# Three attention stages: the product with the values turned round, bias and row extreme in one operation, order of the grouped units

## The reference

```python
# NA: each latent query sees an 8 x 16 window of keys with a position bias, and all 256 context keys
p = softmax_f32(jnp.concatenate([s_win * scale + rpb, s_ctx], axis=-1))
# GQA: each query sees all 1280 keys; 4 heads share one pair of keys and values
p = softmax_f32(concatenate([q @ k.T, q @ k_ctx.T]) * scale)
# FOX: causal over 1024 keys; decay terms ride in extra columns of q and k
out = p @ v        # in all three: probabilities times values, 64 columns per head
```

## Time and profile before

| | us |
|---|---|
| three runs | 4702.28, 4691.91, 4700.87; median 4700.87 |
| profiled execution, its own time | 4704.09 |
| its span | 4702.3 |
| PE busy over the span | 4112.0 (87%) |
| DVE, ACT, POOL busy | 2156.8, 1523.6, 815.8 |

### The profile page before, as it was taken

How to read it: one execution, slowest core, us unless ns; L and a number is a source line. 1 busy time by engine, 2 the same in 40 slices (tenths; PEclk the granted TensorE clock), 3 DMA queues, 4 the chain that set the end, 5 groups by cost and what they waited for, 6 DMA issues and landing times. The chain is left out here.

```text
span 4702.3 us, 74174 instructions
## 1 busy us (share of the span) xinstructions
PE 4112.0 (87%) x29857; PEld 3383.3 (72%) x29857; DVE 2156.8 (46%) x3952; ACT 1523.6 (32%) x3236; POOL 815.8 (17%) x725
## 2 busy tenths in 40 slices
PE   8999797998989985898887879997895988999998
PEld 2789787997889872787776724446794766888786
DVE  3233375344522228677777764475313553111234
ACT  2111254655521117333333350005212553221133
POOL 0000353100100661434444460001000000000000
PEclk9999898999999997999999979998897989999999
DMA  8233432102332566212222050214224132111122
GB/s 321 74 102 115 111 80 60 32 18 92 126 99 92 191 221 250 62 35 49 49 49 49 22 188 25 76 49 170 91 92 165 49 119 72 49 45 49 38 89 69
DMA packets 291264, 439.23 MB, mean 93 GB/s; under 512 B 76980, under 2 KB 210708, under 8 KB 286399
## 3 DMA queue, kind: packets, MB, share of 16 engines
q1 hardware_dynamic: 290664, 429.81, 28.9%
q10 hardware_dynamic: 288, 5.07, 0.3%
HBM read 315.76 MB, written 124.03 MB: 94 GB/s over the span
## 5 line engine op out<-in xcount | busy, mean ns | idle before, releaser
L387 PE MATMUL g_acc<-g_wh,l_x_high 128*128 128x320 f32 (+5 forms) x1824 | 593.5, 325 | 40.2 <-DVE g_wl L53 33.7
L387 PE MATMUL g_acc<-g_wl,l_x_high 128*128 128x320 f32 (+5 forms) x1824 | 591.4, 324 | 0.0
L387 PE MATMUL g_acc<-g_wh,l_x_low 128*128 128x320 f32 (+5 forms) x1824 | 591.0, 324 | 0.0
L387 PEld LDWEIGHTS g_acc<-g_wh,l_x_high 128*128 128x128 f32 x1824 | 347.3, 190 | 48.6 <-DVE g_wl L53 34.3
L387 PEld LDWEIGHTS g_acc<-g_wl,l_x_high 128*128 128x128 f32 x1824 | 348.1, 191 | 2.8
L387 PEld LDWEIGHTS g_acc<-g_wh,l_x_low 128*128 128x128 f32 x1824 | 347.4, 190 | 2.4
L435 DVE COPY g_o<-g_acc 128x320 f32<-128x320 f32 (+6 forms) x120 | 62.7, 524 | 576.9 <-PE g_acc L387 539.4
L411 ACT COPY g_o<-g_acc 128x320 f32<-128x320 f32 (+6 forms) x120 | 54.6, 455 | 772.7 <-PE g_acc L387 730.7
L3088 PE MATMUL ffi_acc<-l4a_x_high,ffi_wh 128*128 128x512 f32 x704 | 274.9, 390 | 11.9 <-DVE ffi_wl L53 11.9
L3088 PE MATMUL ffi_acc<-l4a_x_high,ffi_wl 128*128 128x512 f32 x704 | 274.6, 390 | 0.0
L3088 PE MATMUL ffi_acc<-l4a_x_low,ffi_wh 128*128 128x512 f32 x704 | 274.6, 390 | 0.0
(11 more groups left out here) (508 smaller groups left out, 9572.8 us busy)
## 6 DMA issues: line engine op xcount, KB each, us to landing
scan_F<-s_FE SPq DMA_DIRECT2D x160, 192.0 KB, 3.7
s_FE<-feat_f SPq DMA_DIRECT2D x10, 2304.0 KB, 7.8
ffi_w<-in_w_ffn_in SPq DMA_DIRECT2D x44, 512.0 KB, 3.8
g_cu<-s_U SPq DMA_DIRECT2D x24, 768.0 KB, 5.1
pj_o<-s_O SPq DMA_DIRECT2D x26, 512.0 KB, 4.6
front_w<-in_attn_ada_w SPq DMA_DIRECT2D x8, 1536.0 KB, 12.1
front_w<-in_rec_ada_w SPq DMA_DIRECT2D x8, 1536.0 KB, 12.5
g_wr<-in_w_ffn_out SPq DMA_DIRECT2D x44, 256.0 KB, 2.6
```

Of the source, the lines that this page charges most:

```text
L387: mm = pe.matmul(acc[r][:, 0:it["n"]], left, right, start=(k == 0 and q == 0), stop=(k == kt - 1 and q == 2))
```

## The change

In `mix` the operands change places: 64 columns of values are stationary and the 128 queries of a `probT` tile are streamed. The result lies values-first (64 x 128); tiles of even number add up in partitions 0 to 63 of `po`, those of odd number in partitions 64 to 127. A new `move` copies these 128 x 128 to `oT` in SBUF (ACT in NA and FOX, DVE in GQA), and a new `flip` on PE multiplies `oT` (stationary) with `two`, two identities one above the other: this adds the halves and turns them back to queries x 64, in columns 128 to 191 of the same `po` bank. `normalize` reads these, one unit later than before; `den` and `rden` have four columns instead of two, and `softmax` waits for `normed` of the unit four before.

In `maximum`, units with a bias (NA's large ones, and now all of FOX) use one `tensor_tensor_reduce`: it adds the bias, multiplies by -1, writes `biased` and reduces by minimum. The bias and mask tiles get columns of zeros to cover all keys, and the exponential gets scale -1. In FOX, PE may write the next scores once `maxed` is there, where it waited for `probs`.

In GQA the PE order is late score(w), turning(w-1) of groups 0 and 1, flip(w-2), turning(w-1) of group 2, score(w+1), mix(w-1), and DVE copies group 2 (`on_vector`) between its normalize(w-2) and move(w-1).

```diff
-        den = st.sb("den", [P, 2])
-        rden = st.sb("rden", [P, 2])
+        den = st.sb("den", [P, 4])
+        rden = st.sb("rden", [P, 4])
+        two = st.sb("two", [P, HD])
+        oT = [st.sb(f"oT{i}", [P, P]) for i in range(2)]
...
-            bias = [st.sb(f"bias{i}", [P, 5, 640]) for i in range(2)]
+            bias = [st.sb(f"bias{i}", [P, 5, SMAX]) for i in range(2)]
+        if causal is not None:
+            mask = st.sb("mask", [P, SMAX])
+        if window is not None or causal is not None:
             biased = [st.sb(f"biased{i}", [P, SMAX]) for i in range(2)]
-        if causal is not None:
-            mask = st.sb("mask", [P, P])
...
         def has_bias(w):
-            return window is not None and units[work[w][1]]["bias"] is not None
+            return causal is not None or (window is not None and units[work[w][1]]["bias"] is not None)
+
+        def on_vector(i):
+            return shared and i == 2
+
+        def copied(eng, n):
+            sides = [on_vector(i) for g in groups for i in range(len(g))][:n]
+            eng.wait_ge(turned, len(sides) - sum(sides))
+            if sum(sides):
+                eng.wait_ge(turned_v, sum(sides))
 
         def kv(h):
             return kvs.index(kv_of[h])
+
+        def halves(w):
+            return P if len(units[work[w][1]]["tiles"]) > 1 else HD
...
-                            mm = pe.matmul(po[w % NPO][:, 0:HD], probT[w % 2][:, t, :], v[g % 2][:, u["tiles"][t], :],
-                                           start=(t == 0), stop=(t == len(u["tiles"]) - 1))
+                            half = slice(t % 2 * HD, (t % 2 + 1) * HD)
+                            mm = pe.matmul(po[w % NPO][half, 0:P], v[g % 2][:, u["tiles"][t], :], probT[w % 2][:, t, :],
+                                           start=(t < 2), stop=(t >= len(u["tiles"]) - 2))
                     mm.then_inc(summed, 1)
+
+                def flip(w):
+                    if w == 0:
+                        pe.wait_ge(two_out, 2)
+                    pe.wait_ge(moved, w + 1)
+                    pe.matmul(po[w % NPO][:, P:P + HD], oT[w % 2][0:halves(w), :], two[0:halves(w), :], start=True, stop=True).then_inc(flipped, 1)
...
                         turning(w - 1, (0, 1))
+                        if w >= 2:
+                            flip(w - 2)
+                        turning(w - 1, (2,))
                         if w + 1 < N:
                             score(w + 1)
-                        turning(w - 1, (2,))
                         mix(w - 1)
                 else:
                     for w in range(N + LA):
                             turning(w - LA, (0, 1))
                         if w < N:
                             score(w)
+                        if w > LA:
+                            flip(w - LA - 1)
                         if w >= LA:
                             mix(w - LA)
+                flip(N - 1)
...
-                        act.wait_ge(normed, w - 1)
+                    if w >= 4:
+                        act.wait_ge(normed, w - 3)
                     src = biased[w % 2] if has_bias(w) else scores[w % 2]
-                    nc.scalar.activation(prob[w % 2][:, 0:n], src[:, a:a + n], ACT.Exp, bias=mx[:, w % 2:w % 2 + 1],
-                                         accum_out=den[:, w % 2:w % 2 + 1]).then_inc(probs, 1)
+                    nc.scalar.activation(prob[w % 2][:, 0:n], src[:, a:a + n], ACT.Exp, bias=mx[:, w % 2:w % 2 + 1], scale=-1.0 if has_bias(w) else 1.0,
+                                         accum_out=den[:, w % 4:w % 4 + 1]).then_inc(probs, 1)
...
+                        if on_vector(i):
+                            continue
...
+                def move(w):
+                    act.wait_ge(summed, w + 1)
+                    if w >= 2:
+                        act.wait_ge(flipped, w - 1)
+                    nc.scalar.copy(oT[w % 2][0:halves(w), :], po[w % NPO][0:halves(w), 0:P]).then_inc(moved, 1)
 
                 for w in range(N + LA):
                     if w >= LA:
                         turn(w - LA)
                     if 0 <= w - LA + 1 < N:
                         softmax(w - LA + 1)
+                    if act_moves and w >= LA:
+                        move(w - LA)
...
+                for hb in (slice(0, HD), slice(HD, P)):
+                    dve.tensor_copy(two[hb, :], ident[hb, hb]).then_inc(two_out, 1)
...
+                    dve.memset(mask[:, :], 0.0).then_inc(plain, 1)
                     dve.wait_ge(const_in, 16)
+                if window is not None:
+                    for b in bias:
+                        dve.memset(b[:, :, 0:CTX], 0.0).then_inc(plain, 1)
...
                     if has_bias(w):
-                        dve.wait_ge(bias_ready, 5 * h + u["bias"] + 1)
-                        to = biased[w % 2]
-                        dve.tensor_tensor(to[:, CTX:CTX + 640], src[:, CTX:CTX + 640], bias[h % 2][:, u["bias"], :], ALU.add).then_inc(dve_seq, 1)
-                        link.n += 1
-                        link(dve.tensor_copy(to[:, 0:CTX], src[:, 0:CTX]))
-                        src = to
-                    if causal is not None:
-                        link(dve.tensor_tensor(src[:, n - P:n], src[:, n - P:n], mask[:, :], ALU.add))
+                        if causal is not None:
+                            add = mask[:, SMAX - n:SMAX]
+                        else:
+                            dve.wait_ge(bias_ready, 5 * h + u["bias"] + 1)
+                            add = bias[h % 2][:, u["bias"], :]
+                        dve.tensor_tensor_reduce(out=biased[w % 2][:, 0:n], in0=src[:, a:a + n], in1=add, scale=-1.0, scalar=3e38,
+                                                 op0=ALU.add, op1=ALU.min, accum_out=mx[:, w % 2:w % 2 + 1]).then_inc(maxed, 1)
+                        return
                     dve.tensor_reduce(mx[:, w % 2:w % 2 + 1], src[:, a:a + n], AX.X, ALU.max, negate=True).then_inc(maxed, 1)
...
-                    dve.wait_ge(summed, w + 1)
...
+                    dve.wait_ge(flipped, w + 1)
...
+                    dve.tensor_scalar(o[h // 2 % 2][:, x, h % 2, :], po[w % NPO][:, P:P + HD], rden[:, w % 4:w % 4 + 1], None, ALU.mult).then_inc(normed, 1)
...
+                def turn(w):
+                    if w >= 2:
+                        dve.wait_ge(summed, w - 1)
+                    for i, tl in enumerate(groups[w]):
+                        if on_vector(i):
+                            n = first[w] + i
+                            dve.wait_ge(trans, n + 1)
+                            dve.tensor_copy(probT[w % 2][:, tl[0]:tl[-1] + 1, :],
+                                            pt[n % NPT][:, 0:len(tl) * P].rearrange("p (b t) -> p b t", t=P)).then_inc(turned_v, 1)
 
                 for w in range(N + LA):
                     if w < N:
                         maximum(w)
-                    if w >= LA:
-                        normalize(w - LA)
+                    if w > LA:
+                        normalize(w - LA - 1)
+                    if shared and w >= LA:
+                        turn(w - LA)
+                    if not act_moves and w >= LA:
+                        move(w - LA)
+                normalize(N - 1)
```

More of the change, by code:

```diff
@@ L615, in products, with attention_stage @@
                     mm.then_inc(self.turned, 1)
-def attention_stage(nc, name, ident, K, nk, units, heads, kv_of, q_in, k_in, v_in, o_out, LA, shared, split, table_in=None, window=None, causal=None):
+def attention_stage(nc, name, ident, K, nk, units, heads, kv_of, q_in, k_in, v_in, o_out, LA, shared, split, table_in=None, window=None, causal=None, act_moves=False):
     SMAX = max(sum(n for _, n in u["keys"]) for u in units)
@@ L661, in attention_stage @@
         q_high_out, q_low_out, k_high_out, k_low_out = (st.sem(n) for n in ("q_high_out", "q_low_out", "k_high_out", "k_low_out"))
-        scored, maxed, probs, trans, turned, summed, normed, dve_seq, bias_ready = (st.sem(n) for n in (
-            "scored", "maxed", "probs", "trans", "turned", "summed", "normed", "dve_seq", "bias_ready"))
+        scored, maxed, probs, trans, turned, turned_v, summed, moved, flipped, normed, dve_seq, bias_ready, two_out = (st.sem(n) for n in (
+            "scored", "maxed", "probs", "trans", "turned", "turned_v", "summed", "moved", "flipped", "normed", "dve_seq", "bias_ready", "two_out"))
         work = [(h, x) for h in range(heads) for x in range(NU)]
@@ L737, in _ @@
                 elif causal is not None:
-                    sp.dma_start(mask[:, :], causal).then_inc(const_in, 16)
+                    sp.wait_ge(plain, 1)
+                    sp.dma_start(mask[:, SMAX - P:SMAX], causal).then_inc(const_in, 16)
                 load(1)
@@ L774, in _ @@
                             pool.wait_ge(const_in, 16)
+                            pool.wait_ge(plain, 2)
                         pool.wait_ge(table_loaded[h % 2], 32 * (h // 2 + 1))
@@ L778, in _ @@
```

(21 more changed lines are left out.)

6 lines of the change are left out of this document (3 added, 3 removed).

## The result

The changed kernel takes **4650.4 us** (median of 4 runs, 4645.9 to 4655.9) against 4701.6 for the kernel before on the same chip (4 runs, 4691.9 to 4702.5). The ratio is 0.9896, 95% interval 0.9879 to 0.9914: 51 us or 1.0% faster. The forecast was 4684 within 4634 to 4722, so the direction and the range hold, and the gain is three times the 17 us forecast. The time lies outside the 4668 to 4702 of the preferred case A and inside the 4633 to 4660 of case B; the range held because it took in both.

The account below looks back on a forecast made before the run. PE was taken to bound the three attention stages, with an ACT loop nearly as long in NA and DVE waits between its heads. NA -26, GQA +3 and FOX +7 gave -16, from 4704 to 4688, hence 4684 us at the median; range 4634 to 4722.

Parts of the forecast that it names:

- case A: The preferred sum: column halves overlap, crossings cost 0.35 per unit; 4684 us, 4668 to 4702; chance 0.45 with rival E in it.
- case B: Rival: crossings between full array and column halves cost little, 0 to 0.15 per unit; 4633 to about 4660 us; chance 0.27.
- Mix and crossings: PE per unit: seven tiles' mix 0.86 instead of 1.51, ten 1.18 instead of 2.15; crossings 0.15 in, 0.20 out.
- (n + 1) x 0.107: Forecast mix time in us for n tiles, the second pass of one tile running beside the first of the next.
- GQA: +3 forecast: GQA stage: large units 4.44 instead of 4.52, -5; small units +7; tail +1.
- NA: -26 forecast: NA stage: large units -2.5, seven head boundaries of 9.65 instead of 12.90 -23, start -1, tail +1.
- The loop of ACT and PE: In NA's large units, copies, gap, exponential and transpositions were taken to limit the unit to 3.05 instead of 3.10 us.
- rival E: The fused operation is as slow as its three, 2.28 us in NA; 4695 us; its chance lies within case A's 0.45.
- Move: Copy of 128 x 128, under 0.3 us, free on ACT and on DVE in GQA; uncovered, 19 us in NA.
- +7 forecast: FOX stage: mix, flips and crossings 9.2 against 7.7 us per head, half taken, +6 (0 to +12); tail +1.
- Rival C: In mix the column halves run one after the other, 0.107 us per pass as before; 4807 us, slower; chance 0.10.
- D: Rival: crossings cost 0.45 to 0.60 us per unit, around the flip and mix; 4730 us at 0.60; chance 0.15.

Follow-up runs that it names:

- experiment 5: Changed kernel, but mix gives the first half of a unit's tiles to the lower column half, the rest to the upper, instead of in turns: 4716.1 us, ratio 1.0026.
- experiment 6: Changed kernel with the flip put behind mix's second tile in NA and FOX, so larger units cross twice each way: 4687.0 us, ratio 0.9968.
- experiment 4: Changed kernel with the three VectorE operations (bias add, copy, reduction) put back in NA; FOX keeps the fused one: 4655.4 us, ratio 0.9897.
- Experiment 8: Changed kernel with GQA's next scores ahead of the third group's transpositions again, as in the kernel before: 4634.4 us, ratio 0.9847.
- experiment 1: Kernel before with only the fused VectorE operation for bias or mask and row extreme, in NA and FOX: 4683.9 us, ratio 0.9954.
- Experiment 7: Changed kernel with GQA's third group of transposed tiles copied by ScalarE again instead of VectorE: 4648.2 us, ratio 0.9880.
- experiment 3: Kernel before with the fused bias and extreme plus the exponential's wait for normalize four units back instead of two: 4679.5 us, ratio 0.9949.

## Why the prediction was right, and where its size was wrong

**Mix and crossings, the term that was mis-sized.** Case A named the mechanism: halves in turns overlap (experiment 5 shows it), crossings cost something, and both were in the sum. The size was off in two places. First, (n + 1) x 0.107 holds for odd numbers of tiles and is 0.107 too much for even ones. From mix to what follows it, the timeline after the change shows 0.37 for two tiles in FOX, 0.59 for four, 0.81 for six, 1.03 for eight, and in GQA 1.24 for ten. That is n x 0.107 + 0.16 to 0.17; odd counts take the time of the next even one (three 0.59, five 0.80; seven in NA 1.02), since the last tile has no partner in the other half. The way out, on top of that, is some 0.16; I had 0.20. Second, the way in is 0.05 to 0.11 instead of 0.15. For GQA's ten tiles forecast and measurement stand term by term:

| | forecast | measured |
|---|---|---|
| first transposition to third group | 1.34 | 1.33 |
| third group to mix | 1.24 + 0.15 | 1.30 |
| mix to late scores | 1.18 + 0.20 | 1.24 |
| late scores | 0.33 | 0.34 |
| unit | 4.44 | 4.21 |

The 0.35 of that term measures 0.12 here, that of an NA unit about 0.21 ((0.26 + 1.02) less (0.21 + 0.86)). The difference of the two is the even count: with it set right, the way in and out costs 0.21 to 0.23 in both, between A's 0.35 and the 0 to 0.15 of B. So the time landed in B's 4633 to 4660 without B's price being right; the even counts, and gains that the sum did not have, below, did the rest.

What the crossing is, can be read from one start to the next: 0.21 from the last mix pass (562.90 + 0.81 = 563.71) to the transposition (563.92), and 0.21 from the flip's second pass (562.64 + 0.33 - 0.28 = 562.69) to mix (562.90). The scan stage's 0.21, my nearest row, was right for both directions. The mistake was to add another 0.1 for an uncovered load on each unit. In the changed kernel the flip follows the long passes of the scores or of the transpositions and its load is early; where its neighbours are short, experiment 6 shows the forecast's 0.35 per extra pair.

**GQA: +3 forecast, -15 measured.** Large units: 5 per head at -0.30 (4.51 to 4.21) and 3 at -0.40 on average (4.08, 3.79 and 3.34 from mix to mix before; 3.72, 3.24 and 3.05 after) make -2.7 per head, -22 in all, instead of -5. The two small units of a head: 1.88 + 4.41 before, 2.84 + 4.03 after, +0.58, +5 in all, where I had +7. The other 2 us are at the stage's start and end; from the first scores to the first mix it is 11.90 against 10.50, but 10.84 in experiment 4 with the same code. The prediction's own test ("wrong if GQA changes by more than 20") was not reached, by 5 us.

**GQA's order.** The prediction saw the wait of 0.3 for ACT and booked it, but it did not say that this part of the change costs by itself. Experiment 8 shows it: 16 us.

**NA: -26 forecast, -33 measured, partly by errors that cancel.** The boundary: 9.65 forecast, 9.12 measured. But I multiplied 12.90 by seven, and the trace of before has 11.39 in three of them, without the spell at the lower clock. Sum: -23 forecast, 63.95 - 85.99 = -22.0 measured. What was missing is mostly inside the head, units at 2.93, not 3.05, 6 us over the stage; the rest is at its start, 2.6 shorter (12.78 to 10.14 from the first scores to the second transposition) where I had 1. The loop of ACT and PE that I put at 3.05 isn't one. Its 0.09 between copies and exponential was no part of ACT's work: after the change the exponential starts (562.60) before the copies end (562.71). Experiment 6 confirms that PE sets the pace: NA's units take up the whole 0.35.

**The fused operation.** 1.1 forecast, 1.10 measured; rival E is out. Its worth was spread rightly: the boundary, nothing within a head (experiments 1 and 4). I forecast that half the boundary's gain, 11 us, hangs on it. In NA it is 16.6 alone and 8.6 beside the rest, and most of the difference has a name: at the full clock it is worth 1.17 or 1.08 per head change either way, and alone it also ends the four spells at 1.2 GHz, 6.3 us, which experiment 4 does not have either, without the fused operation.

**Move.** Free in the rows, as forecast: 0.27 on ACT, started after waiting 0.28 for PE; 0.29 on DVE in GQA. No run takes it alone. Experiment 7 shows that the added copy costs next to nothing on either engine.

**FOX.** +7 forecast, -0.1 measured. The fused operation brings -1.6 (experiment 1), and -3.0 with the wait (experiment 3, FOX 166.7); so turned values cost +2.9, not +6, with a spread of 1.5 between profiles. The unit of five tiles shows it: +0.05 in 3.12.

**Rival C** (halves one after the other) is refuted for this order and is real for another: in blocks the kernel is slower than before. The time there was 4716, not 4807: passes of one half cost the 0.107 that C took, but where the blocks meet they overlap, and the crossings are cheaper. **D** is out: way in and out together cost 0.21 to 0.23, not 0.45.

Some 2.6 us of the 51.1 lie outside the three stages; what they are is open. So is why the spells at 1.2 GHz appear at some head changes and not at others: behind an idle of 2.13 at four of seven, behind 1.66 at three of seven, behind 0.96 or less at none.

## What to carry to other kernels

Two column halves double the rate of 64-column products; give the tiles to the halves in turns, since long blocks lose the overlap but where they meet, and count the pairs, not the tiles. A change between full-array and half-array passes costs about 0.1 us here over the distance that the pass before it takes anyway, whichever way (0.21 behind a half-array or a 64-column pass instead of 0.107), and about 0.1 more where the full-array matmul between two such changes is short. When an edit shortens an idle, look at the clock behind it before adding up what edits are worth: part of one gain was a spell at 1.2 GHz. And look for the engine's wait that a new order opens: here the scores put back into PE's wait for a copy, one line moved, are worth a third of what the whole change brought.

## What the runs showed of the hardware that was not expected

- Passes of 128 x 64 weights and 128 streamed columns: 0.054 apart with halves in turns ((1.31 - 0.28) / 19), in truth pairs that start together, one pair every 0.10 to 0.11; 0.108 inside a block of one half ((0.82 - 0.28) / 5), the same as the product the other way round, 128 x 128 weights and 64 columns (0.107). Where two blocks meet, passes further apart than neighbours overlap too: four tiles take 0.59 in turns and 0.60 in blocks of two.
- With halves in turns an odd number of tiles takes, within 0.01 us, the time of the next even one (1.02 for seven, 1.03 for eight).
- Of two 64-column full-array passes (the flip), the second starts 0.05 behind the first where they follow a pass of 384 columns, and 0.15 behind it where they follow half-array passes.
